# Squared norms of the delta rule's queries and keys: from GpSimd squares and products with ones to ScalarE sums over transposes

## The chip, the cores and the metric

The kernel runs on one core of a Trainium2 chip. The metric is the device time of one execution in microseconds. The engines of the core are TensorE (PE in the profile; its weight loads are PEld), VectorE (DVE), ScalarE (ACT), GpSimd (POOL) and SyncE (SP), each with its own queue of instructions, executed in order; they wait for each other through semaphores. TensorE writes to PSUM, the others read and write PSUM or SBUF, GpSimd SBUF alone.

## What is computed

A trunk of two residual layers over 256 tokens of 2048 channels, all in float32. The even layer projects the normalised input to three mixers (a gated delta rule of 8 heads, a long depthwise convolution behind a gated linear unit, and attention to 256 memory tokens), gates them, and projects back; the odd layer does the same with stick-breaking attention. What the change touches is the normalisation of the delta rule's queries and keys:

```python
def l2_norm(x):
    return x * lax.rsqrt(jnp.sum(x * x, axis=-1, keepdims=True) + EPS)

    qkv = jax.nn.silu(causal_depthwise_conv(qkv_a, conv_qkv)).astype(f32)
    q, k, v = [t.reshape(bsz, seq, DN_HEADS, DN_HEAD_DIM) for t in jnp.split(qkv, 3, axis=-1)]
    q = l2_norm(q) * (DN_HEAD_DIM ** -0.5)
    k = l2_norm(k)
    beta = jax.nn.sigmoid(b_a.astype(f32))
    g = -jnp.exp(a_log.astype(f32)) * jax.nn.softplus(a_a.astype(f32) + dt_bias.astype(f32))
    o = gated_delta_rule(q, k, v, beta, g)
```

## The kernel before

**The stream of weights.** All weight matrices are read once, in 432 chunks of 256 rows by 512 columns (512 KB), through six raw buffers. For each chunk ScalarE makes a rounded copy (`whi`, line 824), VectorE the remainder (`wlo`, line 1153), and TensorE twelve matmuls of 128x512 (lines 1497 to 1499: high by high, remainder by high, high by remainder, for two row blocks and two token blocks). `split` (ScalarE's and VectorE's part) of chunk c stands in the plan between chunks c-5 and c-4. A job is a group of chunks that yields 512 output columns; `evac` j copies its result to SBUF on ScalarE (line 851).

**The mixers between the chunks.** `make_plan` puts every step of the mixers into one list, in which the chunks are the clock: a stream of steps has a position in chunks, each step adds a cost in chunks, and the step goes ahead of the chunk at its rounded position. Each engine walks the list and issues its part of each step, so the list is the order of all queues. There is no other scheduler. A step that is not ready holds back everything behind it on its engine.

**The delta rule, group by group.** Heads 0 to 3 are group 0, heads 4 to 7 group 1. The four PSUM banks `mixer0` to `mixer3` (M[0] to M[3]) serve all steps; `take` makes TensorE wait until the last user of a bank has been read. For head h:

- `dnT`: TensorE turns q, k and v to channel order, six transposes into banks 0 and 1 (line 1517, the common helper of all transposes).
- `dnC`: ScalarE multiplies the last tap of the short convolution (line 918), VectorE adds the nine others (line 1227).
- `dnS`: ScalarE's tanh (lines 924, 925) into banks 0 and 1; `dnU`: VectorE's gate product (lines 1235, 1237), after which `ykqv` holds k, q and v. The next `dnT` waits for it.
- `dnB`: GpSimd squares k and q (line 743) into `scr`; TensorE multiplies the squares with ones, four products of one column each (line 1581), into columns 384 to 387 of bank 2, and turns k's first half and v's halves back to token order (three transposes); ScalarE copies them to `tok` (line 932), VectorE copies the four norms to `nrm` (line 1243).
- `dnV` for a whole group: VectorE adds a constant (line 1248), ScalarE takes the logarithm (line 936), VectorE makes the exponents (lines 1252 to 1265), ScalarE the exponential (line 938). Each of the two functions has a table load.
- `dnR`: TensorE turns the exponents, VectorE copies them to `rows`. `dnG`: TensorE's products of k and q and the decays (lines 1599 to 1607), ScalarE's exponential (line 946), VectorE's product (line 1282).
- `d4x` and `d4y`: the inverse by seven doubling levels, for two pairs of heads in turn (numbers 0 to 6 and 7 to 13 in group 0, 14 to 20 and 21 to 27 in group 1); GpSimd masks (line 763), TensorE multiplies (lines 1619, 1634, 1635), VectorE reads the banks (lines 1290 and 1291 for the first level, 1304 and 1305 later).
- `d5a` to `d5e`, `d6`, `gate` and `d7`: the outputs, their norm, their gate, and two transposes back (ScalarE's copy, line 988).

Beside it run `glu` (ScalarE's tanh, line 993, VectorE's product, line 1341), its transposes `gT`, the taps of the long convolution `conv` on VectorE (lines 1355 and 1358, four a step), and `za`, the gate of the delta rule (line 910, line 1215).

Of the kernel before, what the change touches and what calls it, by code (L numbers as in the profile page):

```python
# [129 lines left out]
DN_STEP = 3.5  # L130
# [13 lines left out]
def make_plan(last_job):  # L144
# [18 lines left out]
    def deltanet(g):  # L163
# [126 lines left out]
def prog(nc, x, mem, vecs, w, a_log, dt_bias, out, last_job=len(JOBS)):  # L290
# [4 lines left out]
    with ctx:  # L295
# [140 lines left out]
        s_sq = sem("dn_squares")  # L436
        s_back = sem("dn_kv_transposed_back")
        s_tok = sem("dn_kv_by_token")
        s_np = sem("dn_norms_summed")
        s_nrm = sem("dn_norms_copied")  # L440
# [99 lines left out]
        def banks(step, i):  # L540
            if step == "xt":
                return [i % 3 if 8 <= i < F_OB else i % 4]
            if step in ("mqT", "mkT"):
                return [i % 2]
            if step == "mao":
                return [2 + i % 2]
            if step == "d4y":
                return [] if i % 7 == 0 else ([1, 2] if i % 7 < 6 else [2])
            return {"first": [0], "vec": [3], "ba": [0], "bat": [1], "bas": [2], "dnT": [0, 1], "dnB": [2], "dnR": [1], "dnG": [0, 1],
                    "d4x": [0],  # L550
                    "d5a": [0], "d5b": [1], "d5c": [2], "d5d": [0], "d5e": [1], "d7": [2], "gT": [3], "zT": [3],
                    "lnm": [3], "lns": [3], "mas": [0], "mat": [1], "sbT": [0], "sbz": [1], "sbo": [2]}.get(step, [])
# [4 lines left out]
        def read(step, i):  # L557
# [3 lines left out]
                    "dnB": (s_nrm, i + 1), "dnR": (s_rows, i + 1), "dnG": (s_aq, i + 1),  # L561
# [134 lines left out]
        def _(gp):  # L696
# [105 lines left out]
            steps = {"rstd": do_rstd, "dnB": do_dnB, "dnG": do_dnG, "d4x": do_d4x, "lnc": do_lnc, "d6": do_d6, "sbk": do_sbk, "sbn": do_sbn,  # L802
# [6 lines left out]
        def _(sc):  # L809
# [311 lines left out]
            def do_xload(b):  # L1121
# [6 lines left out]
                     "za": do_za, "dnC": do_dnC, "dnS": do_dnS, "dnB": do_dnB, "dnV": do_dnV, "dnG": do_dnG, "d4x": do_d4x,  # L1128
# [13 lines left out]
        def _(ve):  # L1142
# [327 lines left out]
            def do_sbo(h):  # L1470
# [9 lines left out]
                     "dnU": do_dnU, "dnB": do_dnB, "dnV": do_dnV, "dnR": do_dnR, "dnG": do_dnG, "d4x": do_d4x,  # L1480
# [9 lines left out]
        def _(pe):  # L1490
# [85 lines left out]
            def do_dnB(h):  # L1576
                pe.wait_ge(s_silu, 2 * h + 2)
                take("dnB", h)
                pe.wait_ge(s_sq, h + 1)
                for a in range(4):  # L1580
                    ins = mm(M[2][:, 384 + a:385 + a], scr[:, 128 * a:128 * a + 128], ones[:, 0:1], start=True, stop=True)
                ins.then_inc(s_np, 1)
# [3 lines left out]
                turn(M[2][:, 256:384], y[:, 2, 128:256]).then_inc(s_back, 1)  # L1586

# [187 lines left out]
            def do_sbo(h):  # L1775
# [9 lines left out]
                     "dnT": do_dnT, "dnB": do_dnB, "dnR": do_dnR,  # L1785
# [49 lines left out]
```

## Time and profile before

| | us |
|---|---|
| median of three runs | 1425.14 |
| lowest and highest | 1423.98, 1425.86 |
| the profiled execution | 1425.36 |
| its span in the trace | 1423.6 |

| engine | busy us | share of the span |
|---|---|---|
| TensorE, matmuls | 1398.6 | 98% |
| TensorE, weight loads | 1167.6 | 82% |
| VectorE | 896.5 | 63% |
| ScalarE | 758.7 | 53% |
| GpSimd | 136.2 | 10% |

The span is the time from the first to the last instruction in the trace; the execution's own time is 1.8 us longer. In the chain that ended last TensorE has 91% of the span, the three matmul lines of the chunks 26% each. A share of busy time is an average over the whole span; the steps of the delta rule lie between 100 and 530 us.

### The profile page before, as it was taken

How to read it: one execution, taken by the hardware profiler on the slowest of the kernel's cores; microseconds unless marked ns; L12 is line 12 of the kernel's file. 1: busy time of each engine (PE TensorE's matmuls, PEld its weight loads, DVE VectorE, ACT ScalarE, POOL GpSimd, SP SyncE). 2: the span in 40 equal slices, each digit the busy share in tenths (PEclk: the TensorE clock that was granted, in tenths of full speed). 3: DMA queues.
4: the chain of work that ended last, by engine and by line, in shares of the span. 5: the costliest groups of instructions: out<-in, count | busy, mean ns of one | idle time of the engine just before them, and what ended most of it. 6: DMA issues, size and time to landing. Idle time of an engine off the chain costs nothing.

```text
span 1423.6 us, 18074 instructions
## 1 busy us (share of the span) xinstructions
PE 1398.6 (98%) x6811; PEld 1167.6 (82%) x6811; DVE 896.5 (63%) x1297; ACT 758.7 (53%) x1175; POOL 136.2 (10%) x135
## 2 busy tenths in 40 slices
PE   7999999999999999999999999999999999999998
PEld 5888889888889888878888788888888888888887
DVE  4447697777786789865566553655554645656563
ACT  4545633455533564666444545765765756655441
POOL 3001222110322010000000120020020020000000
PEclk9999999999999999999999999999999999999999
DMA  7555533455433486546455565455464564553552
GB/s 261 184 186 163 163 120 104 133 163 161 150 118 104 135 272 215 163 132 213 140 160 177 173 215 176 140 184 183 152 194 160 178 192 163 177 177 105 192 192 75
DMA packets 124847, 236.42 MB, mean 166 GB/s; under 512 B 9648, under 2 KB 10073, under 8 KB 124761
## 3 DMA queue, kind: packets, MB, share of 16 engines
q1 hardware_dynamic: 122585, 231.07, 51.2%
q10 hardware_dynamic: 2176, 4.19, 0.9%
q8 instruction: 55, 0.90, 0.3%
q14 instruction: 31, 0.25, 0.1%
HBM read 233.14 MB, written 2.10 MB: 165 GB/s over the span
## 4 chain that ended last, share of the span: by engine, by line
PE 91%; DVE 4%; ACT 2%; issue 1%; SPq 1%; DMA 0%; POOL 0%; DVEq 0%; ACTq 0%
PE job L1497 26%; PE job L1499 26%; PE job L1498 26%; PE mixer L1517 4%; PE mixer L1619 2%; PE mixer L1635 1%; PE mixer L1634 1%; DVE wlo L1153 1%; PE mixer L1749 1%; PE mixer L1729 1%; ACT whi L824 1%; DVE cvr L1358 1%; DVE reg L1227 1%; PE mixer L1767 0%; PE mixer L1780 0%
## 5 line engine op out<-in xcount | busy, mean ns | idle before, releaser
L1497 PE MATMUL job<-whi,xhi 128*128 128x512 f32 x1728 | 695.2, 402 | 0.2 <-DVE wlo L1153 0.2
L1153 DVE TENSOR_TENSOR wlo<-raw,whi 128x1024 fp32r<-128x1024 f32 x432 | 527.6, 1239 | 246.6 <-ACT whi L824 244.2
L1499 PE MATMUL job<-whi,xlo 128*128 128x512 f32 x1728 | 677.0, 392 | 0.0
L1498 PE MATMUL job<-wlo,xhi 128*128 128x512 f32 x1728 | 675.5, 391 | 0.0
L824 ACT ACTIVATE whi<-raw 128x1024 fp32r<-128x1024 f32 x432 | 445.4, 1056 | 135.9 <-PE job L1499 127.8
L1499 PEld LDWEIGHTS job<-whi,xlo 128*128 128x128 f32 x1728 | 325.7, 188 | 70.6
L1498 PEld LDWEIGHTS job<-wlo,xhi 128*128 128x128 f32 x1728 | 326.5, 189 | 62.7
L1497 PEld LDWEIGHTS job<-whi,xhi 128*128 128x128 f32 x1728 | 326.2, 189 | 62.7 <-issue 0.6
L1358 DVE SCALAR_TENSOR_TENSOR cvr<-cvr,vt 128x255 f32<-128x255 f32 (+14 forms) x240 | 117.3, 549 | 0.0
L851 ACT ACTIVATE proj<-job,rstd 128x512 f32<-128x512 f32 x80 | 50.5, 686 | 43.0 <-PE job L1499 35.5
L955 ACT ACTIVATE reg<-mixer 128x512 f32<-128x512 f32 x24 | 14.4, 599 | 93.0 <-PE mixer L1619 93.0
L1169 DVE TENSOR_TENSOR hid<-hid,job 128x512 f32<-128x512 f32 x48 | 30.8, 682 | 50.1 <-PE job L1499 50.1
L763 POOL TENSOR_TENSOR reg<-hid,mix 128x512 f32<-128x512 f32 x28 | 39.5, 1410 | 120.6 <-DVE mix L1305 87.3
L1517 PE MATMUL mixer<-ident,proj 128*128 128x128 f32 x256 | 42.3, 273 | 4.3 <-DVE proj L1419 2.5
L732 POOL TENSOR_TENSOR brs<-bss,mhalf 128x16 f32<-128x16 f32 x4 | 15.2, 3807 | 308.7 <-DVE bss L1449 308.7
L1455 DVE SCALAR_TENSOR_TENSOR scr<-mixer,scr 128x384 f32<-128x384 f32 x16 | 8.9, 558 | 56.4 <-ACT scr L1109 56.4
L1517 PEld LDWEIGHTS mixer<-ident,proj 128*128 128x128 f32 x256 | 32.0, 141 | 14.7 <-issue 3.3
L1107 ACT ACTIVATE scr<-mixer 128x384 f32<-128x384 f32 x16 | 7.9, 492 | 60.0 <-PE mixer L1767 60.0
L1227 DVE SCALAR_TENSOR_TENSOR reg<-mixer,vt,reg 128x255 f32<-128x255 f32 (+2 forms) x72 | 28.8, 473 | 11.2 <-ACT reg L918 11.1
L1635 PE MATMUL mixer<-mix,reg 128*128 128x64 f32 x192 | 34.9, 273 | 0.0
L861 ACT ACTIVATE xhi<-mixer,vt 128x256 fp32r<-128x256 f32 x48 | 20.0, 471 | 25.4 <-PE mixer L1517 25.4
L1174 DVE SCALAR_TENSOR_TENSOR xlo<-mixer,vt,xhi 128x256 fp32r<-128x256 f32 x48 | 20.8, 478 | 14.3 <-ACT xhi L861 14.3
(253 smaller groups left out, 976.1 us busy)
## 6 DMA issues: line engine op xcount, KB each, us to landing
raw<-in_od_w_in_dram SPq DMA_DIRECT2D x160, 512.0 KB, 4.4
raw<-in_ev_w_in_dram SPq DMA_DIRECT2D x144, 512.0 KB, 3.7
raw<-in_ev_w_out_dram SPq DMA_DIRECT2D x48, 512.0 KB, 4.6
raw<-in_od_w_out_dram SPq DMA_DIRECT2D x48, 512.0 KB, 4.4
raw<-in_w_mem_kv_dram SPq DMA_DIRECT2D x32, 512.0 KB, 4.1
hid<-in_x_dram SPq DMA_DIRECT2D x4, 512.0 KB, 7.6
reg<-in_mem_dram ACTq DMA_DIRECT2D x4, 512.0 KB, 6.0
hid<-in_x_dram ACTq DMA_DIRECT2D x4, 512.0 KB, 7.9
```

Source lines behind the costliest of these rows:

```text
L763: nc.gpsimd.tensor_tensor(ofx[:, par, :, :], aq[:, 4 * par:4 * par + 4, 0, :], level[:, l, :].unsqueeze(1).broadcast_to([128, 4, 128]), AL ...
L824: act(whi[:, c % RING, :, :], raw[:, c % RAWS, :, :], ACT.Copy).then_inc(s_hi, 1)
L851: ins = act(dst, pj[j % 2][t][:, :], ACT.Copy, scale=rstd[:, src, t:t + 1])
L1153: vec.tensor_tensor(wlo[:, c % RING, :, :], raw[:, c % RAWS, :, :], whi[:, c % RING, :, :].bitcast(F32), ALU.subtract).then_inc(s_lo, 1)
L1169: ins = vec.tensor_tensor(v, v, pj[j % 2][t][:, :], ALU.add)
L1227: vec.scalar_tensor_tensor(out=y[:, r:], in0=dn_source(c)[:, 0:S - r], scalar=vt[:, col:col + 1], in1=y[:, r:], op0=ALU.mult, op1=ALU.add) ...
L1358: ins = vec.scalar_tensor_tensor(out=c[:, d:], in0=gsrc[:, 0:S - d], scalar=vt[:, col:col + 1], in1=c[:, d:], op0=ALU.mult, op1=ALU.add)
L1497: mm(out_, xh, hi, start=first, stop=False)
L1498: mm(out_, xh, lo, start=False, stop=False)
L1499: return mm(out_, xl, hi, start=False, stop=last)
L1517: return nc.tensor.transpose(dst, src, ident[:, :])
L1635: ins = mm(m2, ofx[:, par, m, :], t1[:, :, 1, :], start=True, stop=True)
```

## The change

`dnB` is split. TensorE no longer multiplies squares with ones and GpSimd no longer squares. `dnB` on TensorE is the three transposes alone, and ScalarE, ahead of its copy to `tok`, squares k's first half where it lies in bank 2 and sums along the row into `nrm` (`accum_out`). A new step `dnE` turns the other three halves (k's second, q's both) into bank 2, and ScalarE squares and sums each. VectorE's copy of the norms is gone. In the plan `dnB` of a head no longer stands in front of the next head's `dnT` but one step earlier, `dnE` takes its place, and the cost of `dnU` and the wait at the group's end are shorter, so that what follows in the delta rule stands one chunk earlier in group 0 and one to two chunks earlier in group 1. The numbers of `nrm` keep their meaning.

```diff
@@ make_plan, deltanet(g) @@
         for h in range(h0, h0 + 4):
-            s += [(("dnT", h), .2), (("dnC", h), 1.2), (("dnS", h), .9), (("dnU", h), DN_STEP - 2.1)]
+            s += [(("dnT", h), .2), (("dnC", h), 1.2)]
             s += [(("dnB", h - 1), .1)] if h > h0 else []
-        s += [("wait", 1), (("dnB", h0 + 3), 1), (("dnV", g), 2), (("dnR", g), 2.2)]
+            s += [(("dnS", h), .9), (("dnU", h), DN_STEP - 2.3)]
+            s += [(("dnE", h - 1), .1)] if h > h0 else []
+        s += [("wait", .5), (("dnB", h0 + 3), 1), (("dnE", h0 + 3), .5), (("dnV", g), 2), (("dnR", g), 2.2)]
         s += [(("dnG", h), 1) for h in range(h0, h0 + 4)]
@@ who has read a bank @@
-                    "dnB": (s_nrm, i + 1), "dnR": (s_rows, i + 1), "dnG": (s_aq, i + 1),
+                    "dnB": (s_tok, i + 1), "dnE": (s_nrm, i + 1), "dnR": (s_rows, i + 1), "dnG": (s_aq, i + 1),
@@ GpSimd @@
-            def do_dnB(h):
-                gp.wait_ge(s_silu, 2 * h + 2)
-                if h:
-                    gp.wait_ge(s_np, h)
-                k = ykqv[:, h % 4, 0:2, :]
-                nc.gpsimd.tensor_tensor(scr[:, 0:512].rearrange("p (c s) -> p c s", c=2), k, k, ALU.mult).then_inc(s_sq, 1)
-
@@ ScalarE @@
                 sc.wait_ge(s_ss, 1)
+                act(scr[:, 0:128], M[2][:, 0:128], ACT.Square, accum_out=nrm[:, h, 0:1])
                 act(tok[:, h % 4, :, :], M[2][:, 0:384].rearrange("p (c n) -> p c n", c=3), ACT.Copy).then_inc(s_tok, 1)
+
+            def do_dnE(h):
+                sc.wait_ge(s_kq, h + 1)
+                for a in range(1, 4):
+                    ins = act(scr[:, 128 * a:128 * a + 128], M[2][:, 128 * a - 128:128 * a], ACT.Square,
+                              accum_out=nrm[:, h, a:a + 1])
+                ins.then_inc(s_nrm, 1)
@@ VectorE @@
-            def do_dnB(h):
-                ve.wait_ge(s_np, h + 1)
-                ve.wait_ge(s_tok, h + 1)
-                vec.tensor_copy(nrm[:, h, :], M[2][:, 384:388]).then_inc(s_nrm, 1)
-
@@ TensorE @@
                 take("dnB", h)
-                pe.wait_ge(s_sq, h + 1)
-                for a in range(4):
-                    ins = mm(M[2][:, 384 + a:385 + a], scr[:, 128 * a:128 * a + 128], ones[:, 0:1], start=True, stop=True)
-                ins.then_inc(s_np, 1)
                 y = ykqv[:, h % 4, :, :]
                 turn(M[2][:, 0:128], y[:, 0, 0:128])
                 turn(M[2][:, 128:256], y[:, 2, 0:128])
                 turn(M[2][:, 256:384], y[:, 2, 128:256]).then_inc(s_back, 1)
+
+            def do_dnE(h):
+                take("dnE", h)
+                y = ykqv[:, h % 4, :, :]
+                turn(M[2][:, 0:128], y[:, 0, 128:256])
+                turn(M[2][:, 128:256], y[:, 1, 0:128])
+                turn(M[2][:, 256:384], y[:, 1, 128:256]).then_inc(s_kq, 1)
```

What the new order is, at three places. First ScalarE at the end of group 0, from the work on head 3's norms to the first copy of a GLU transpose. `hln` holds the logarithms, `ex` the factors, `proj` in the row with 1024 columns the GLU's gate, `whi<-raw` a chunk's rounded copy. Before:

```order
L932 ACTIVATE hid<-mixer2 128x384
L993 ACTIVATE proj<-proj 128x1024
L824 ACTIVATE whi<-raw 128x1024
L936 ACT_TABLE_LOAD
L936 ACTIVATE hln<-hln 128x16
L938 ACT_TABLE_LOAD
L938 ACTIVATE ex<-ei 128x32
L997 ACTIVATE cvr<-mixer3 128x256
```

and with the change:

```order
L932 ACTIVATE scr,nrm<-mixer2 128x128 x3
L938 ACT_TABLE_LOAD
L938 ACTIVATE hln<-hln 128x16
L940 ACT_TABLE_LOAD
L940 ACTIVATE ex<-ei 128x32
L995 ACTIVATE proj<-proj 128x1024
L818 ACTIVATE whi<-raw 128x1024
L999 ACTIVATE cvr<-mixer3 128x256
```

The GLU's tanh has moved from ahead of the logarithm and the exponential to behind them. TensorE's GLU transposes stand one chunk behind head 3's last transposes in both.

Second, VectorE from the product of `dnG` with which `za` shares its place to the first read of the inverse (`mix<-ident,mixer0`), group 0. `hid<-mixer0,hid` is a head's `dnG`, `cvr<-cvr,vt` are taps of the long convolution. Before:

```order
L1282 TENSOR_TENSOR hid<-mixer0,hid 128x512
L1215 SCALAR_TENSOR_TENSOR mix<-mix,proj 128x2x512
L1358 SCALAR_TENSOR_TENSOR cvr<-cvr,vt 128x252 x2
L1358 SCALAR_TENSOR_TENSOR cvr<-cvr,vt 128x251 x2
L1153 TENSOR_TENSOR wlo<-raw,whi 128x1024
L1282 TENSOR_TENSOR hid<-mixer0,hid 128x512
L1358 SCALAR_TENSOR_TENSOR cvr<-cvr,vt 128x250 x2
L1358 SCALAR_TENSOR_TENSOR cvr<-cvr,vt 128x249 x2
L1153 TENSOR_TENSOR wlo<-raw,whi 128x1024
L1290 TENSOR_TENSOR mix<-ident,mixer0 128x512
```

and with the change:

```order
L1279 TENSOR_TENSOR hid<-mixer0,hid 128x512
L1217 SCALAR_TENSOR_TENSOR mix<-mix,proj 128x2x512
L1355 SCALAR_TENSOR_TENSOR cvr<-cvr,vt 128x252 x2
L1355 SCALAR_TENSOR_TENSOR cvr<-cvr,vt 128x251 x2
L1155 TENSOR_TENSOR wlo<-raw,whi 128x1024
L1355 SCALAR_TENSOR_TENSOR cvr<-cvr,vt 128x250 x2
L1355 SCALAR_TENSOR_TENSOR cvr<-cvr,vt 128x249 x2
L1155 TENSOR_TENSOR wlo<-raw,whi 128x1024
L1287 TENSOR_TENSOR mix<-ident,mixer0 128x512
```

The last head's `dnG` has moved ahead of `za`, out of this stretch; the taps and remainders in it are the same. In the plan `d4x` 0 and 7 keep their chunks (51, 52), `d4x` 1 moves from chunk 54 to 53.

Third, VectorE in group 1, from the last exponents (`ei<-hln`) to the product of head 4 (`hid<-mixer0,hid`). Before:

```order
L1265 TENSOR_SCALAR ei<-hln 128x8
L1215 SCALAR_TENSOR_TENSOR mix<-mix,proj 128x2x512
...
L1277 TENSOR_SCALAR nks<-ex 128x8
L1358 SCALAR_TENSOR_TENSOR cvr<-cvr,vt 128x228 x2
L1358 SCALAR_TENSOR_TENSOR cvr<-cvr,vt 128x227 x2
L1153 TENSOR_TENSOR wlo<-raw,whi 128x1024
L1358 SCALAR_TENSOR_TENSOR cvr<-cvr,vt 128x226 x2
L1153 TENSOR_TENSOR wlo<-raw,whi 128x1024
L1282 TENSOR_TENSOR hid<-mixer0,hid 128x512
```

and with the change:

```order
L1262 TENSOR_SCALAR ei<-hln 128x8
L1355 SCALAR_TENSOR_TENSOR cvr<-cvr,vt 128x234 x2
...
L1274 TENSOR_SCALAR nks<-ex 128x8
L1217 SCALAR_TENSOR_TENSOR mix<-mix,proj 128x2x512
L1355 SCALAR_TENSOR_TENSOR cvr<-cvr,vt 128x230 x2
L1355 SCALAR_TENSOR_TENSOR cvr<-cvr,vt 128x229 x2
L1155 TENSOR_TENSOR wlo<-raw,whi 128x1024
L1355 SCALAR_TENSOR_TENSOR cvr<-cvr,vt 128x228 x2
L1355 SCALAR_TENSOR_TENSOR cvr<-cvr,vt 128x227 x2
L1155 TENSOR_TENSOR wlo<-raw,whi 128x1024
L1279 TENSOR_TENSOR hid<-mixer0,hid 128x512
```

`za` has moved behind the copies of `dnR`, and the two last taps (128x226) now follow the product.

## Rows read from the trace of the kernel before

**Rows 1.** The page's busy shares, us (share of the span) xinstructions.

```profile
PE 1398.6 (98%) x6811; PEld 1167.6 (82%) x6811; DVE 896.5 (63%) x1297; ACT 758.7 (53%) x1175; POOL 136.2 (10%) x135
```

**Rows 2.** The chain that ended last: start us, us, what; head 0's norms.

```profile
123.15 0.79 PE mixer L1581 x8
123.94 1.04 PE mixer L1517 x9
```

**Rows 3.** Timeline, 150 to 172: start, us, engine, line, op, tiles [idle before <-releaser].

```profile
153.79 0.49 ACT L932 ACTIVATE hid<-mixer 128x384 f32<-128x384 f32 x1 [2.48 <-PE mixer L1517]
...
155.26 1.23 DVE L1341 SCALAR_TENSOR_TENSOR proj<-proj 128x1024 f32<-128x1024 f32 x1 [0.72 <-ACT proj L993]
...
156.20 1.28 ACT L936 ACT_TABLE_LOAD   x1
...
156.54 0.44 PE L1517 MATMUL mixer<-ident,proj 128*128 128x128 f32 x2
...
157.74 0.22 ACT L936 ACTIVATE hln<-hln 128x16 f32<-128x16 f32 x1 [0.26 <-DVE hln L1248]
```

**Rows 4.** Timeline of ScalarE at a pair of squares with sums.

```profile
276.71 0.31 ACT L983 ACTIVATE hid<-hid 128x128 f32<-128x128 f32 x1 [1.92 <-DVE hid L1316]
...
277.31 0.35 ACT L973 ACTIVATE scr<-mixer,ex 128x128 f32<-128x128 f32 x1
```

**Rows 5.** Timeline of TensorE: the transposes of heads 0 and 1.

```profile
101.46 0.82 PE L1517 MATMUL mixer<-ident,proj 128*128 128x128 f32 x6
...
111.41 0.85 PE L1517 MATMUL mixer<-ident,proj 128*128 128x128 f32 x6 [0.96 <-DVE reg L1237]
```

**Rows 6.** Timelines of TensorE, then VectorE: `dnG` 3, `d4x` 0 and 7, group 0.

```profile
181.72 1.02 PE L1599 MATMUL mixer<-reg 128*128 128x256 f32 x4
...
183.16 0.45 PE L1497 MATMUL job<-whi,xhi 128*128 128x512 f32 x1
...
185.95 1.05 PE L1619 MATMUL mixer<-ident,reg 128*128 128x128 f32 x8
...
190.53 1.13 PE L1619 MATMUL mixer<-ident,reg 128*128 128x128 f32 x8 [0.80 <-DVE mix L1291]
...
189.71 0.68 DVE L1291 TENSOR_TENSOR mix<-ident,reg 128x512 f32<-128x512 f32 x1
...
194.61 0.68 DVE L1291 TENSOR_TENSOR mix<-ident,reg 128x512 f32<-128x512 f32 x1
```

**Rows 7.** Timelines of ScalarE, VectorE, TensorE: from `dnB` 7 to `dnG` 5.

```profile
355.11 1.26 ACT L851 ACTIVATE proj<-job,rstd 128x512 f32<-128x512 f32 x2
...
357.35 1.23 DVE L1153 TENSOR_TENSOR wlo<-raw,whi 128x1024 fp32r<-128x1024 f32 x1 [0.38 <-ACT whi L824]
...
364.88 1.31 DVE L1215 SCALAR_TENSOR_TENSOR mix<-mix,proj 128x1024 f32<-128x1024 f32 x1 [1.60 <-ACT mix L910]
...
374.77 0.81 DVE L1358 SCALAR_TENSOR_TENSOR cvr<-cvr,vt 128x226 f32<-128x226 f32 x2
...
376.64 0.68 DVE L1282 TENSOR_TENSOR hid<-mixer,hid 128x512 f32<-128x512 f32 x1
...
358.08 0.53 PE L1517 MATMUL mixer<-ident,reg 128*128 128x128 f32 x3
...
377.46 1.10 PE L1599 MATMUL mixer<-reg 128*128 128x256 f32 x4 [0.85 <-DVE hid L1282]
```

**Rows 8.** Waits of TensorE: line <- waited for: us in total, times, longest.

```profile
PE mixer L1517 <- ACT mix L988: 0.7, 1, 0.7
```

**Rows 9.** Timeline of TensorE; then stretches: busy of engines, PEclk, DMA share, GB/s.

```profile
25.25 0.66 PE L1517 MATMUL mixer<-ident,hid 128*128 128x128 f32 x2 [3.51 <-DVE xlo L1174]
...
634.02 0.44 PE L1517 MATMUL mixer<-ident,proj 128*128 128x128 f32 x2 [2.53 <-DVE proj L1419]
...
25.00:31.00 6.00, 5.75 (x15) 4.50 (x16) 3.62 (x6) 1.91 (x4) 0.00 (x0) 0.50 1.05 387
635.00:640.00 5.00, 5.00 (x18) 3.94 (x17) 4.64 (x5) 3.68 (x8) 0.00 (x0) 0.66 0.56 173
```

More of the change, by code:

```diff
@@ L435, in prog @@
         s_silu = sem("dn_silu")
-        s_sq = sem("dn_squares")
         s_back = sem("dn_kv_transposed_back")
         s_tok = sem("dn_kv_by_token")
-        s_np = sem("dn_norms_summed")
-        s_nrm = sem("dn_norms_copied")
+        s_kq = sem("dn_kq_transposed_back")
+        s_nrm = sem("dn_norms_summed")
         s_lnq = sem("dn_log_norms")
@@ L548, in banks @@
                 return [] if i % 7 == 0 else ([1, 2] if i % 7 < 6 else [2])
-            return {"first": [0], "vec": [3], "ba": [0], "bat": [1], "bas": [2], "dnT": [0, 1], "dnB": [2], "dnR": [1], "dnG": [0, 1],
+            return {"first": [0], "vec": [3], "ba": [0], "bat": [1], "bas": [2], "dnT": [0, 1], "dnB": [2], "dnE": [2], "dnR": [1], "dnG": [0, 1],
                     "d4x": [0],
@@ L800, in do_sbn @@
                                             ALU.mult).then_inc(s_sbn, 1)
-            steps = {"rstd": do_rstd, "dnB": do_dnB, "dnG": do_dnG, "d4x": do_d4x, "lnc": do_lnc, "d6": do_d6, "sbk": do_sbk, "sbn": do_sbn,
+            steps = {"rstd": do_rstd, "dnG": do_dnG, "d4x": do_d4x, "lnc": do_lnc, "d6": do_d6, "sbk": do_sbk, "sbn": do_sbn,
                      "mqs": lambda i: mq_power(i, order[i]), "mks": lambda i: mq_power(4 + i, order[4 + i])}
@@ L1127, in _ @@
                      "baw": do_baw, "ba": do_ba, "bat": do_bat,
-                     "za": do_za, "dnC": do_dnC, "dnS": do_dnS, "dnB": do_dnB, "dnV": do_dnV, "dnG": do_dnG, "d4x": do_d4x,
+                     "za": do_za, "dnC": do_dnC, "dnS": do_dnS, "dnB": do_dnB, "dnE": do_dnE, "dnV": do_dnV, "dnG": do_dnG, "d4x": do_d4x,
                      "d5a": do_d5a, "d5b": do_d5b, "d5c": do_d5c, "d5d": do_d5d, "d5e": do_d5e, "d7": do_d7,
@@ L1479, in _ @@
                      "za": do_za, "dnC": do_dnC,
-                     "dnU": do_dnU, "dnB": do_dnB, "dnV": do_dnV, "dnR": do_dnR, "dnG": do_dnG, "d4x": do_d4x,
+                     "dnU": do_dnU, "dnV": do_dnV, "dnR": do_dnR, "dnG": do_dnG, "d4x": do_d4x,
                      "d4y": do_d4y, "d5c": do_d5c, "d5e": do_d5e, "d6": do_d6, "gate": do_gate, "glu": do_glu,
@@ L1784, in _ @@
             steps = {"chunk": do_chunk, "xt": do_xt, "vec": do_vec, "ba": do_ba, "bat": do_bat, "bas": do_bas,
-                     "dnT": do_dnT, "dnB": do_dnB, "dnR": do_dnR,
+                     "dnT": do_dnT, "dnB": do_dnB, "dnE": do_dnE, "dnR": do_dnR,
                      "dnG": do_dnG, "d4x": do_d4x, "d4y": do_d4y, "d5a": do_d5a, "d5b": do_d5b, "d5c": do_d5c,
```

## The prediction

> **What bounds the kernel now.** First the page's busy shares: TensorE is busy for 1398.6 of 1423.6 us [rows 1]; the engine whose queue never empties is the bound, and anything else counts only where TensorE comes to wait for it. So I read the waits of TensorE next, then the chain that ended last for what its instructions cost in that queue, then the timelines of ScalarE, VectorE and TensorE at the few places where the new order leaves TensorE less time between asking and needing. "Chunk n" is the group of twelve weight matmuls between two mixer steps; it costs 2.79 us (183.16 to 185.95) [rows 6]. The profiled execution took 1425.4 us, 0.2 above the median of the three runs; the sum is made against it.
>
> **Part 1: work on TensorE.** Removed for each of eight heads: the four products with ones, eight instructions in 0.79 us of the chain [rows 2]. Added: three more transposes. Nine stand in 1.04 us [rows 2], 0.35 for three; as they now stand alone more often, I take 0.38. The upper bound is two in 0.44, so 0.66 for three [rows 3]. Gain: 8 x (0.79 - 0.38) = 3.3 us, between 1.0 and 3.5. GpSimd's eight squares and VectorE's eight copies of the norms go too; TensorE never waited for the copies, so I cost their loss at nothing. The loads of the memory input and of x, issued from ScalarE's queue, move a chunk or two forward together with the steps around them; TensorE never waits for them, cost nothing; the queue of the weight loads keeps its order.
>
> **Part 2: ScalarE's squares, and who queues behind them.** ScalarE gets 32 squares with a sum. Two such squares with their read-outs take 276.71 to 277.31, 0.60 us, so 0.30 each [rows 4]; the bound above is instruction plus read-out end to end, 0.5. In most places they fall into ScalarE's idle time. The dear place is the end of the first group. Before, the copy of head 3 was followed by the GLU's tanh, then VectorE's GLU product; TensorE's first GLU transpose came at 156.54, 0.05 us after the product ended at 155.26 + 1.23 = 156.49 [rows 3]. There is no slack. Now ScalarE does the three squares, a table load, the logarithm, a second load and the exponential, and only then the tanh; VectorE likewise has its exponents ahead of the GLU product (the order of both engines shows it). TensorE's distance from head 3's last transposes to the GLU transpose is one chunk, as before. So the tanh is later by 0.90 (squares) + 2 x 1.28 (loads) + 2 x 0.22 (logarithm, exponential) - 0.49 (the copy that stood there) = 3.4 us [rows 3, 4]. With 0.14 us from VectorE's end to TensorE's start (189.71 + 0.68 to 190.53 [rows 6]) and the 0.05 slack, TensorE waits 3.5 us, between 2.6 (squares for nothing) and 4.1 (squares at 0.5).
>
> The row shows a load of 1.28 us at 156.20, ended by 157.48, and the logarithm at 157.74 behind a VectorE step [rows 3]. The Trainium skill, "ScalarE: Activation LUTs", section "What ACT_TABLE_LOAD costs", adds a drain of some 1.38 us to every load; by it the wait would be 2.8 us longer. The trace leaves 0.26 us behind the load, against that rule, and the sum goes by the row.
>
> **Part 3: less room between transposes.** dnT of heads 3 and 7 now comes three chunks after that of the head before, not four. One such spacing exists: dnT 0 at 101.46, dnT 1 at 111.41 with 0.96 us of waiting [rows 5]: the convolution, tanh and product round trip takes 9.95, TensorE's own work 8.99. In the new places TensorE also has three groups of three transposes, 8.99 + 3 x 0.38 = 10.13. The round trip starts after dnE (0.38), and the squares outlast dnT's own transposes by 0.90 - (1.04 - 0.38) = 0.24, so it takes 10.57. Wait 0.44, twice: 0.9 us, between 0 and 1.9 (the 0.96 each).
>
> **Part 4: first products of the inverse, first group.** Step d4x 7 waited 0.80 us at 190.53 for VectorE to read the bank of d4x 0 [rows 6]. Now dnG 3 lies a chunk earlier, so TensorE asks 1.44 us sooner (181.72 to 183.16), and VectorE is freed of only one product ahead, 0.68 [rows 6, 7]: wait 0.80 + 1.44 - 0.68 = 1.56. Then d4x 1, before two chunks behind d4x 7, stands one behind: TensorE is there after 1.13 + 2.79 = 3.92 us, VectorE reads that bank 4.90 after the former (189.71 to 194.61) [rows 6]; wait 0.98. Together 2.5 against 0.8: 1.7 us more, between 0 and 2.4.
>
> **Part 5: second group's decay matrices.** dnG 5 waited 0.85 us at 377.46 for the product of dnG 4 [rows 7]. Now dnV 1 follows dnE 7 at once, and everything to dnG 5 comes a chunk sooner after the last transposes: TensorE asks at 377.46 - 0.85 - 358.08 - 2.79 = 15.7 us after their start. VectorE: 0.52 (transposes, hand-over) + 0.90 (squares) + 3.00 (loads, logarithm, exponential) + 2.24 (job result and split on ScalarE until VectorE's split, 355.11 to 357.35) = 6.7; then its queue to dnG 4, which ran 364.88 to 376.64, 11.76 us without a gap, now without the last two taps of 0.81: 17.6. From that product's start to TensorE 0.82: 18.4. Wait 2.7, 1.8 more than before, between 0 and 2.4 more.
>
> **Part 6: back.** The last output transposes, which stood two steps in one chunk and waited 0.7 us [rows 8], get a chunk each: 0.7 us gained.
>
> **Part 7: TensorE's clock.** Behind a wait of 2.53 us the granted clock was 0.66 over the stretch 635 to 640, so partly at the lower of the two levels (1.2 GHz), price 0.34 x 5 = 1.7 us; behind one of 3.51 us it was 0.50 over 25 to 31, price 0.50 x 6 = 3.0 [rows 9]. Part 2's wait of 3.5 us is like the larger; I take the middle of the two prices, 2.4 us. Part 5's 2.7 us is barely above 2.53; I count nothing and keep 1.7 for the range.
> The Trainium skill has the rule, "TensorE: Matmul & The Clock Gate", section "Why this matters for your kernels": an idle gap between bursts of matmuls puts the engine back to half rate. It speaks against this change, and both rows agree with it.
>
> Sum: -3.3 + 3.5 + 0.9 + 1.7 + 1.8 - 0.7 + 2.4 = 6.3. 1425.4 + 6.3 = **1431.7 us**.
>
> **Rivals.**
> (a) *The shorter queue wins.* Price: 3.3 + 0.7 less of TensorE's time, 1425.4 - 4.0 = 1421.4. It needs the GLU product to be ready within 1.2 us of TensorE's asking (4.0 - 1.2 = 2.8, the bound of "faster"); up to there the change gains. For it: TensorE is 98% busy and really gets less work, and VectorE no longer stands in wait for the norms. Against it: the queue order at the GLU step is fixed, and its two loads alone are 2.6 us. Chance 0.08.
> (b) *One wait, one gain.* Only part 2's wait comes, parts 3 to 5 are covered since VectorE is freed of its blocking copies, and the clock holds: 1425.4 - 4.0 + 3.5 = 1424.9; with the clock's smaller price 1426.6. For it: the waits of 0.8 to 1.0 us are small against 2.79 us a chunk. Against it: VectorE's stretches in parts 4 and 5 have no gap that a copy caused. Chance 0.20.
> (c) *The clock falls twice*, after parts 2 and 5, at 3.0 and 1.7: 1425.4 + 3.9 + 4.7 = 1434.0. Chance 0.12.
> (d) *A table load holds ScalarE for longer than its instruction shows*, say once more its own 1.28 us: two loads on the way, at part 2 and at part 5, 4 x 1.28 = 5.1 more, 1425.4 + 6.3 + 5.1 = 1436.8. The 0.26 us in the row speaks against it. Chance 0.02.
> This is the mechanism of the drain in the Trainium skill, "ScalarE: Activation LUTs", weighed above.
> That the change doesn't do what it says can be excluded by the order: products and GpSimd squares are gone, and ScalarE has as many table loads as before.
>
> **The numbers.** The forecast has 0.58, (a) 0.08, (b) 0.20, (c) 0.12, (d) 0.02. A measurement tells 0.2%, 2.8 us, from no change, so "same" is 1422.3 to 1428.0. (a) is faster, (b) is same, the rest slower: 0.08, 0.20, 0.72. The range: all low ends with the smaller price of the clock give 1425.4 - 3.5 + 2.6 - 0.7 + 1.7 = 1425.5, the foot; it leaves out (a) and the lower half of (b). All high ends give 1425.4 - 1.0 + 4.1 + 1.9 + 2.4 + 2.4 - 0.7 + 4.7 = 1439.2, which hardly come together; 1437 takes in (c) and most of what is above it.
>
> **What would show it.** In the changed profile: a wait of TensorE's first GLU transpose for VectorE's product of about 3.5 us near 155; a clock window under 1.0 behind it; dnT 3 and dnT 7 waiting some 0.4 us for VectorE's gate product; two waits for the inverse's first copies near 190; one of 2.7 us at dnG 5; no wait at the output transposes; 32 squares at 0.3 us on ScalarE. If the GLU wait is under 1 us, the forecast falls; if it is there and the total is still at 1425, parts 3 to 5 were covered.

## The result, and the profile of the changed kernel

| | us |
|---|---|
| changed kernel, median of seven executions | 1429.41 (1428.58 to 1433.86) |
| kernel before, beside it | 1425.14 |
| ratio | 1.0041, 95% interval 1.0031 to 1.0052 |
| changed kernel, the profiled execution | 1428.66, span 1426.7 |

The change costs 4.3 us, 0.4%. The forecast was 1431.7 in a range of 1425.5 to 1437.0. The page's busy shares [rows 1]:

```profile
PE 1395.1 (98%) x6771; PEld 1162.2 (81%) x6771; DVE 894.5 (63%) x1289; ACT 766.9 (54%) x1239; POOL 126.9 (9%) x127
```

TensorE is busy for 3.5 us less and the kernel is slower, so the whole loss lies in the time in which it stands idle: 31.6 us of the span against 25.0 before. The view of TensorE's waits (line, line waited for, us in total, times, longest) has:

```profile
PE mixer L1514 <- DVE proj L1338: 3.6, 1, 3.6
PE mixer L1514 <- DVE reg L1239: 2.9, 4, 1.2
PE mixer L1599 <- DVE hid L1279: 2.8, 1, 2.8
PE mixer L1619 <- DVE mix L1288: 2.7, 2, 1.7
...
PE mixer L1514 <- DVE mix L1395: 1.1, 1, 1.1
PE mixer L1514 <- DVE proj L1416: 0.7, 1, 0.7
PE mixer L1514 <- ACT mix L990: 0.6, 1, 0.6
```

The same waits before (the line numbers there are a few off): GLU no wait, `dnT` 1.4 in two, decay matrices 0.85, inverse 0.80, the `mix` of line 1395 none, the late `proj` 2.53 [rows 9]. The last row, 0.6 for ScalarE's `mix`, is the wait of `dnB` 4 for bank 2 (at 329.00), which was 0.61 before; the output transposes' 0.7 [rows 8] is gone. The GLU place, which answers to [rows 3], in the timeline (start, us, engine, line):

```profile
151.36 0.28 ACT L932 ACTIVATE scr<-mixer 128x128 f32<-128x128 f32 x1 [1.39 <-PE mixer L1514]
...
151.63 0.27 ACT L932 ACTIVATE scr<-mixer 128x128 f32<-128x128 f32 x1
...
151.88 0.28 ACT L932 ACTIVATE scr<-mixer 128x128 f32<-128x128 f32 x1
...
152.26 1.28 ACT L938 ACT_TABLE_LOAD   x1
...
153.56 0.21 ACT L938 ACTIVATE hln<-hln 128x16 f32<-128x16 f32 x1
...
153.79 1.28 ACT L940 ACT_TABLE_LOAD   x1
...
155.09 0.23 ACT L940 ACTIVATE ex<-ei 128x32 f32<-128x32 f32 x1
155.22 1.04 ACT L995 ACTIVATE proj<-proj 128x1024 f32<-128x1024 f32 x1
156.29 1.32 DVE L1338 SCALAR_TENSOR_TENSOR proj<-proj 128x1024 f32<-128x1024 f32 x1 [1.60 <-ACT proj L995]
...
157.67 0.44 PE L1514 MATMUL mixer<-ident,proj 128*128 128x128 f32 x2 [3.59 <-DVE proj L1338]
```

Read it from the bottom: TensorE waits 3.59 us for VectorE's product, that for ScalarE's tanh, and the tanh starts when both table functions and three squares are through. From the first square to the tanh ScalarE hardly pauses, 3.86 us. The second load starts 0.02 us behind the logarithm, the logarithm 0.02 behind the first load: no hidden time behind either. The other waits in TensorE's timeline (`dnT` 3, 5 and 7; `d4x` 7 and 1; `dnG` 5), answering to [rows 5 to 7]:

```profile
132.67 0.84 PE L1514 MATMUL mixer<-ident,proj 128*128 128x128 f32 x6 [0.37 <-DVE reg L1239]
...
192.10 1.13 PE L1619 MATMUL mixer<-ident,reg 128*128 128x128 f32 x8 [1.66 <-DVE mix L1288]
...
197.01 1.13 PE L1619 MATMUL mixer<-mix,reg 128*128 128x128 f32 x8 [1.04 <-DVE mix L1288]
...
315.82 0.85 PE L1514 MATMUL mixer<-ident,proj 128*128 128x128 f32 x6 [1.24 <-DVE reg L1239]
...
339.45 0.85 PE L1514 MATMUL mixer<-ident,proj 128*128 128x128 f32 x6 [0.36 <-DVE reg L1239]
...
376.24 1.10 PE L1599 MATMUL mixer<-reg 128*128 128x256 f32 x4 [2.80 <-DVE hid L1279]
```

The row at 315.82 is `dnT` 5, which the forecast had left out. The clock, in stretches (start:end, length, busy of the engines, PEclk):

```profile
20.00:31.00 11.00, 8.35 (x37) 6.64 (x36) 5.26 (x8) 5.21 (x9) 0.00 (x0) 0.84 1.03 384
31.00:370.00 339.00, 329.24 (x1714) 276.46 (x1712) 233.66 (x388) 177.90 (x333) 34.05 (x36) 1.00 0.49 149
370.00:390.00 20.00, 17.20 (x85) 14.12 (x84) 13.76 (x21) 8.32 (x15) 7.83 (x10) 0.91 0.51 152
390.00:1420.00 1030.00, 1025.34 (x4888) 853.51 (x4887) 632.36 (x860) 566.72 (x870) 72.18 (x43) 1.00 0.53 168
```

In this execution the clock stayed at 2.4 GHz behind the GLU wait, and also near 635, where it fell before and where the wait is now 0.7 us. It was at 1.2 GHz for part of the time behind `dnG` 5.

### The profile page after: what moved, and what is told of

Read it like the earlier page. It is cut to its first block, busy times and chain, and to the rows that moved or that the text cites. A ratio compares the mean times of both kernels' runs of the same rounds, so it can differ in the third digit from the quotient of the medians.

```text
span 1426.7 us, 18027 instructions
## 1 busy us (share of the span) xinstructions
PE 1395.1 (98%) x6771; PEld 1162.2 (81%) x6771; DVE 894.5 (63%) x1289; ACT 766.9 (54%) x1239; POOL 126.9 (9%) x127
## 4 chain that ended last, share of the span: by engine, by line
PE 90%; DVE 5%; ACT 2%; SPq 1%; issue 1%; DMA 0%; POOL 0%; DVEq 0%; ACTq 0%
PE job L1494 26%; PE job L1496 26%; PE job L1495 25%; PE mixer L1514 4%; PE mixer L1619 2%; DVE wlo L1155 2%; PE mixer L1635 1%; PE mixer L1634 1%; PE mixer L1749 1%; PE mixer L1729 1%; DVE reg L1229 1%; DVE cvr L1355 1%; ACT whi L818 1%; PE mixer L1767 0%; PE mixer L1780 0%
## 5 line engine op out<-in xcount | busy, mean ns | idle before, releaser
L1355 DVE SCALAR_TENSOR_TENSOR cvr<-cvr,vt 128x255 f32<-128x255 f32 (+14 forms) x240 | 114.2, 535 | 0.0
```

Source lines behind the costliest of these rows:

```text
L1355: ins = vec.scalar_tensor_tensor(out=c[:, d:], in0=gsrc[:, 0:S - d], scalar=vt[:, col:col + 1], in1=c[:, d:], op0=ALU.mult, op1=ALU.add)
```

## Experiments

Two theories stood against each other: the loss is the sum of four waits that the order brings (the forecast), or the new method itself, ScalarE's squares, is what costs. In the diffs `move(a, b)` takes step a out of the finished plan and puts it ahead of b, and `put(a, c)` puts it behind chunk c. Each ratio is to the kernel before run beside the experiment: its median was 1424.84 us (27 executions) for the first four and 1424.57 us (15) for the four behind them.

**One wait alone: the GLU step ahead of head 3's squares.**

```diff
+    move(("glu", 0), ("dnE", 3))
```

> The changed kernel with one move in the plan: glu 0 (ScalarE's tanh, VectorE's product) stands ahead of dnE 3 and dnV 0 instead of behind them. Theory of the waits: TensorE's 3.6 us of waiting at the first GLU transpose go, nothing takes their place, the other waits stay (two at the gate products of about 0.4, 1.7 and 1.0 at the inverse, 2.8 at dnG 5): 1429.4 - 3.6 = 1425.8 us, and the executions above 1431 us are gone. Rival, the clock: the loss is mostly the granted clock that falls behind a wait; the fall behind dnG 5 stays, and the time stays at 1428 or above. Rival, hidden anyway: what is gained at the GLU comes back as a longer wait at dnR, dnG or the inverse within the next ten chunks, time 1429.

Measured: 1424.45 us (1423.25 to 1424.98), ratio to before 0.9997 (0.9989 to 1.0006). One step moved past three squares and two table functions gives back 5.0 us between the medians, and no execution of eleven is above 1425.0. The GLU row is gone from TensorE's waits; the others stand where they were:

```profile
PE mixer L1519 <- DVE reg L1244: 3.0, 4, 1.3
PE mixer L1604 <- DVE hid L1284: 2.8, 1, 2.8
PE mixer L1624 <- DVE mix L1293: 2.7, 2, 1.7
```

In the two profiled executions the gain is 1426.7 - 1422.9 = 3.8 us, the wait (3.6) and nothing of the clock, since it had not fallen there. That the medians give 1.2 more is the first sign that it does fall there in other executions.

**The method alone: ScalarE's sums with all other steps at their old places.**

```diff
@@ make_plan, deltanet(g): the streams of before @@
+    for h, b, e in ((0, 33, 34), (1, 37, 38), (2, 39, 40), (3, 41, 42), (4, 87, 88), (5, 91, 92), (6, 93, 94), (7, 95, 96)):
+        if (b, h) not in ((33, 0), (37, 1), (87, 4), (91, 5)):
+            put(("dnB", h), b)
+        put(("dnE", h), e)
```

> The method of the change (four squares with sums on ScalarE, six transposes, no products with ones, no GpSimd squares) with the plan of the kernel before for all other steps. dnB 0, 1, 4, 5 keep their chunks, dnB 2, 3, 6, 7 come one or two chunks sooner, each dnE stands one chunk behind its dnB, dnE 3 behind glu 0. Theory of the waits: TensorE gets 3.3 us less work and has the waits of the kernel before (0.96, 0.80, 0.85, 0.7): 1425.1 - 3.3 = 1421.8 us. Rival, the method costs: the squares and the second hand-over on ScalarE delay the splits and the gate products, and the time is 1425 or above, with new waits at dnT.

Measured: 1420.98 us (1420.60 to 1423.58), ratio 0.9977 (0.9968 to 0.9986). In the old order the new method is worth 3.9 us; with the new order that gain is lost and 4.3 us more. All four waits of the forecast are back at their old size:

```profile
PE mixer L1522 <- DVE proj L1424: 2.5, 1, 2.5
PE mixer L1522 <- ACT scr L940: 1.8, 2, 0.9
...
PE mixer L1522 <- DVE reg L1247: 1.4, 2, 1.0
...
PE mixer L1607 <- DVE hid L1287: 0.9, 1, 0.9
PE mixer L1627 <- DVE mix L1296: 0.8, 1, 0.8
```

The second row is new, and two of its kind: `dnB` 2 and `dnB` 6 want bank 2 while the squares of the head before are not done.

**The order alone: before's method in the changed plan.** GpSimd's squares and the products with ones stay, `dnE` is an empty step, and the plan is the changed one.

> The kernel before (GpSimd squares, products with ones) in the changed plan, in which dnE does nothing. Theory of the waits: TensorE's work is as before, the norms are there a chunk sooner than in the changed kernel, so the GLU wait is only about 1.2 us, that at dnG 5 under 1 and those at dnT 3 and 7 near 0; the waits at the inverse (1.7 and 1.0) and the gain at the output transposes do not depend on the squares and stay: 1425.1 + 1.2 + 1.9 - 0.7 - 0.3 = 1427 us. Rival, the plan alone: the waits belong to the plan and none to the squares; then all of them stay and 3.3 us of TensorE's work come on top: 1432.7 us.

Measured: 1425.38 us (1425.04 to 1426.36), ratio 1.0006 (0.9997 to 1.0015). The wait of the inverse stayed at its full size and that of the GLU step came near the expected 1.2. At `dnG` 5, where less than 1 was expected, it is 1.4:

```profile
PE mixer L1621 <- DVE mix L1293: 2.7, 2, 1.7
...
PE mixer L1519 <- DVE reg L1239: 2.2, 2, 1.2
PE mixer L1519 <- DVE proj L1343: 1.5, 1, 1.5
...
PE mixer L1601 <- DVE hid L1284: 1.4, 1, 1.4
...
PE mixer L1519 <- DVE proj L1421: 0.7, 1, 0.7
```

The time is 1.6 us under the expectation, and the last row gives the likely reason: the late wait is 0.7 here as in the changed kernel, not 2.5. The order has a gain in its tail that the forecast had put at nothing. It also shows that the two halves of the change do not add up: the order alone costs nothing, the method alone gains 3.9, together they lose 4.3. The method puts squares ahead of the table functions in a place where the order has just put those ahead of the tanh. This kernel and the changed one have the same plan, so their difference is what the method does in it. From chunk 24 to 128 the changed kernel, in an execution whose clock did not fall there, takes 403.11 us against 401.63 here, while TensorE's waits in that stretch sum to 12.6 against 7.8 us (2.1 more at the GLU step, 1.4 at `dnG` 5, 0.7 at `dnT` 3 and 7, 0.6 at `dnB` 4). So in the changed plan the method saves TensorE 3.3 us of work, adds 4.8 us of waits, and in most executions adds a fall of the clock as well.

**One cost doubled: every square of `dnE` twice.**

```diff
                 for a in range(1, 4):
+                    act(reg[:, 2944 + 128 * a:3072 + 128 * a], M[2][:, 128 * a - 128:128 * a], ACT.Square,
+                        accum_out=wnrm[:, h, a:a + 1])
                     ins = act(scr[:, 128 * a:128 * a + 128], M[2][:, 128 * a - 128:128 * a], ACT.Square,
```

> The changed kernel, with dnE's three squares done twice (the extra three write to a place that nobody reads): 0.9 us more on ScalarE in each dnE. Theory of the waits: each wait behind dnE grows by 0.9: GLU 3.6 to 4.5, gate products 0.37 to 1.3 twice, dnG 5 2.8 to 3.7, the inverse unchanged; 1429.4 + 3.6 = 1433.0 us. Rival: ScalarE's time is not on the path of the waits (the table loads and the order alone make them), and the time stays within 1 us of 1429.4. The clock may add 1.7 to 3 us in single executions in both.

Measured: 1433.62 us (1432.82 to 1434.50), ratio 1.0062 (1.0049 to 1.0076).

```profile
PE mixer L1517 <- DVE reg L1242: 4.4, 4, 1.3
PE mixer L1517 <- DVE proj L1341: 4.4, 1, 4.4
...
PE mixer L1602 <- DVE hid L1282: 2.8, 1, 2.8
...
PE mixer L1602 <- DVE rows L1274: 0.6, 1, 0.6
```

The expectation was 1433.0. The GLU wait grows by 0.8 us, and the three extra squares hold ScalarE for 0.8 there (1.67 us from the first square to the table load, against 0.90): at this place ScalarE's queue counts one for one. The wait at `dnG` 5 was expected at 3.7 and stayed at 2.8. The last row is where the rest went: `dnG` 4 now waits 0.6 us for the copied rows, one step ahead. VectorE's queue shifted as a whole, as the forecast had it, but TensorE had only a little room left before an earlier step met it. 0.6 + 2.8 = 3.4 is near the 3.7. The `dnT` waits grew by 1.5, from 2.9 to 4.4. In all the waits grew by 2.9 us, not by 3.6, and the median by 4.2. That the total met the expectation is therefore partly chance; the profiled execution has a fall of the clock at both places (0.89 in 154 to 170 and in 374 to 390), where the one of 1428.66 has one.

**Three short waits taken out of the old order.** The kernel with the old places, and

```diff
+    move(("dnE", 1), ("dnS", 3))
+    move(("dnE", 5), ("dnS", 7))
+    move(("dnB", 4), ("chunk", 88))
+    move(("d7", 7), ("conv", 56))
```

> ScalarE's sums in the old plan (as in the run with the old places), with three short waits taken away by order alone: the three squares of heads 1 and 5 stand ahead of the next head's tanh on ScalarE (TensorE waited 0.93 and 0.90 us for them, since they stood behind a tanh that itself waited for VectorE), head 4's transposes stand behind those of head 6 (0.66), and the last output transpose has a chunk of its own (0.7). Theory (a wait of TensorE is all that these orders cost): 1421.0 - 1.8 - 0.7 - 0.7 = 1417.8 us, the rows gone from TensorE's waits. Rival (the squares ahead of the tanh delay the gate product, 0.9 us each, and the next transposes wait instead): 1419.5 to 1421, with new waits for the gate product's register.

Measured: 1418.75 us (1418.22 to 1419.70), ratio 0.9957 (0.9945 to 0.9970). It is 0.9 us above the expected 1417.8. The rows for `scr` and ScalarE's `mix` are gone. The two waits for squares and that of `dnB` 4 gave their time back (chunks 39, 93 and 87 are 1.1, 1.1 and 0.65 us shorter). The output transpose in a chunk of its own gave nothing: chunk 137 is 1.1 us shorter, and chunks 138 to 146 are 1.1 longer together, with a new wait of 0.3 for VectorE's `xlo`. This is what was in the way of the squares, in ScalarE's timeline of the kernel with the old places:

```profile
140.23 0.60 ACT L926 ACTIVATE mixer<-reg 128x512 f32<-128x512 f32 x1 [2.71 <-DVE reg L1237]
...
141.07 0.26 ACT L940 ACTIVATE scr<-mixer 128x128 f32<-128x128 f32 x1
```

ScalarE stood idle for 2.71 us ahead of a tanh, and for the last 1.8 us of it the data of the squares behind it was ready (TensorE's `dnE` 1 stands at 137.91, 0.49 us). A ready instruction behind one that waits is what the new order cures. The squares' length has a part in it too: they start at 141.07, TensorE asks for the bank at 141.15, and its wait of 0.93 is the time that they take.

**The tail a chunk earlier.** The same kernel, and `lnc` 6 to `lno` 7 with `zT` 8 to 15 (the norm and the output transposes of the long convolution, chunks 148 to 170) one chunk earlier, as the changed plan has them.

> The same, and in addition the steps of the long convolution's norm and its output transposes (chunks 148 to 170) stand one chunk earlier, as the change has them and the plan before has not. My prediction gave this shift nothing. In the changed kernel TensorE's wait for VectorE's scaled keys near 635 us was 0.7 instead of 2.5 us, and a new one of 1.1 us stood near 580. Theory (the shift is what shortened the late wait, because VectorE is done with the work of those steps before the keys' squares come): 0.7 to 1.8 us less than the kernel beside it, so 1416.0 to 1417.1, and less often a fall of the clock at 635 (1.7 us when there is one). Rival (it came from elsewhere, for instance from loads that moved with the second group): the wait of 2.5 stays and the two kernels agree within 0.5 us.

Measured: 1417.38 us (1416.68 to 1417.89), ratio 0.9947 (0.9934 to 0.9959). It is the fastest version, 7.2 us under the kernel before and 12 under the changed one's first median. The late wait of 2.5 is gone from the rows altogether; one of 0.5 stands at `mix`. So the shift of the tail is the cause of the late gain, not the loads or the second group. The median gain is 1.4 us, inside the expected 0.7 to 1.8. The mechanism, read from ScalarE's timeline of before:

```profile
628.54 0.42 ACT L1018 ACTIVATE cvr<-cvr 128x256 f32<-128x256 f32 x1 [1.62 <-DVE cvr L1388]
...
629.81 0.40 ACT L1047 ACTIVATE scr<-proj 128x256 f32<-128x256 f32 x1
```

The squares of the keys (`scr<-proj`) stand right behind `lno` 7 (`cvr<-cvr`), which waits 1.62 us for VectorE. In the changed kernel that `lno` comes 2.5 us earlier, counted from the start of chunk 174, and the squares 1.6 earlier. Once more a step in wait held back a ready one.

**The queue ahead of `dnG` 5 shortened.** The first experiment's kernel, and

```diff
+    move(("za", 1), ("chunk", 100))
+    for q in (("conv", 31), ("lnc", 2), ("lnc", 3)):
+        move(q, ("chunk", 102))
```

> The changed kernel with the GLU step ahead of head 3's squares (1424.45 us), and VectorE's queue ahead of head 4's product in group 1 shortened by 2.8 us: the delta rule's gate step stands behind that product, one convolution step stands two chunks later. TensorE's wait of 2.8 us at the second decay matrices should go. Theory with the clock (in the profiled execution it fell for 3.4 us right behind this wait, price 1.7): 1424.5 - 2.8 - 1.7 = 1420.0, no fall near 375. Theory without the clock (it falls elsewhere or as often as before): 1421.7. Rival (VectorE's moved work comes due at once behind it, at the third decay matrices or the GLU transposes of group 1): 1423 to 1424.5.

Measured: 1422.99 us (1422.34 to 1423.15), ratio 0.9986 (0.9977 to 0.9995).
My edit was only half of what I had meant. `conv` 31 already stood behind the product, so that only the gate step (1.2 us) left the queue, and TensorE's wait for the product went from 2.8 to 1.6, not to nothing. The median fell by 1.5, of which 1.2 are this wait; the profiled executions differ by 2.6, and this one had no fall of the clock behind 31 us, where the first experiment's had one behind its 2.8 (0.91 in 374 to 390). Both theories named numbers for a wait that was gone, so neither is settled by this; how the clock's share varies is what the next runs show.

**The changed kernel itself, four executions more with a profile.** The seven times of the result fell into two groups, so what differs between executions of one program was the question.

> The changed kernel itself, unaltered, for more executions and a second profile, because its seven times so far fall into two groups, 1428.6 to 1429.4 at a mean granted clock of 0.996 to 0.997 and 1431.6 to 1433.9 at 0.992 to 0.995. If the clock falls behind its waits in some executions and not in others, times again spread over 1428 to 1434, a lower mean clock goes with a longer time at 1.7 us for each 3.4 us at half clock, and the second profile may show the fall behind the GLU wait near 158 us that the first did not. If the spread came from anything else, long and short executions have the same mean clock. Median 1429 to 1431.

> The changed kernel once more, one profiled execution. Its twelve timed executions lie between 1427.7 and 1433.9 us with mean granted clocks from 0.998 down to 0.992; the two profiled ones (0.997 and 0.998) had no fall behind the 3.6 us GLU wait, one of them had one behind the 2.8 us wait. Theory (the clock falls behind a given wait in some executions only, each fall some 3.4 us at half clock): an execution of 1431 us or more shows two to four more falls, behind the GLU wait near 158, the waits of the inverse near 192 or the decay matrices near 377; one of 1429 us or less shows none or one of these. Rival (a different cause, spread over the whole span): no more than two falls in a long execution.

> The same kernel and the same question as the run before it: where the granted clock falls in a third execution with a profile.

> The same kernel and the same question again: where the granted clock falls in a further execution with a profile.

Measured in the first: median 1431.47 us (1427.73 to 1432.33), ratio 1.0045 (1.0031 to 1.0059), the profiled execution being the shortest. The median is a little above the expected 1429 to 1431, and a lower mean clock goes with a longer time, 0.998 at 1427.73 down to 0.992 at 1433.55, as expected. The other three: 1431.26, 1432.48 and 1433.55. The waits of TensorE agree to 0.1 us in all of them (GLU 3.6, decay matrices 2.8, inverse 2.7), but for that on the input at the start. The stretches from 154 to 170 and from 374 to 390 do not. In the execution of 1427.73:

```profile
154.00:170.00 16.00, 12.39 (x63) 9.93 (x62) 8.04 (x17) 8.71 (x14) 7.26 (x12) 1.00 0.48 141
374.00:390.00 16.00, 13.22 (x71) 10.95 (x70) 11.29 (x16) 6.86 (x12) 8.62 (x10) 1.00 0.56 165
```

in that of 1431.26:

```profile
154.00:170.00 16.00, 12.39 (x51) 9.61 (x51) 8.05 (x17) 8.20 (x12) 7.23 (x12) 0.89 0.42 129
374.00:390.00 16.00, 13.21 (x60) 10.60 (x59) 12.65 (x17) 5.91 (x10) 6.65 (x9) 0.89 0.43 123
```

and in that of 1433.55:

```profile
154.00:170.00 16.00, 12.39 (x47) 9.57 (x46) 7.79 (x17) 8.08 (x12) 7.19 (x12) 0.79 0.38 117
374.00:390.00 16.00, 13.20 (x54) 10.54 (x53) 12.13 (x18) 5.80 (x11) 6.68 (x9) 0.79 0.43 125
```

The column to read is the granted clock (1.00, 0.89, 0.79), and with it the count of matmuls: TensorE is busy for the same 12.39 us, but issues 63, 51 and 47. The starts of chunks in the trace give the price. From chunk 40 to 48 (around the GLU wait) and from 96 to 104 (around `dnG` 5):

| execution, us | 40 to 48 | 96 to 104 | PEclk there |
|---|---|---|---|
| 1427.73 | 30.77 | 31.74 | 1.00, 1.00 |
| 1428.66 | 30.74 | 33.32 | 1.00, 0.89 |
| 1431.26 | 32.34 | 33.24 | 0.89, 0.89 |
| 1432.48 | 33.24 | 34.68 | 0.79, 0.79 |
| 1433.55 | 33.28 | 34.75 | 0.79, 0.79 |

A stretch at 0.89 costs 1.5 to 1.6 us, one at 0.79 costs 2.5 to 3.0. The two places together explain 0, 1.6, 3.1, 5.4 and 5.5 us. What is left is the clock at the start, which fell for longer in the executions of 1427.73, 1431.26 and 1433.55 (0.9 to 1.0 us at chunk 24): without both, the five times are 1426.9, 1427.1, 1427.2, 1427.0 and 1427.1. The falls at these two waits, with the start, are the whole spread of six microseconds. By its own sign (no more than two falls in a long execution) my rival was not refuted, since each long one has exactly two; it is out because these two leave at most 0.3 us unexplained. Of the theory two things were wrong: behind the waits of the inverse the clock never fell, and a fall is not always of one length, since 0.79 stands for twice the time at half clock that 0.89 does. What decides in a single execution whether the clock falls, no run here shows.

## Why the prediction was right, and where it was not

The forecast was 1431.7; the median was 1429.4, in the executions taken later 1431.5. Steps in the prediction's order, in the profiled execution of 1428.66 where nothing else is said:

| part | forecast | measured |
|---|---|---|
| 1, TensorE's work | -3.3 | -3.3 (against before's method in the same plan); busy time -3.5, with the clock in it |
| 2, GLU wait | +3.5 | +3.59 |
| 3, `dnT` 3 and 7 | +0.9 | +0.7; `dnT` 5 +0.8 |
| 4, inverse (1.56 and 0.98 against 0.80) | +1.7 | +1.9 (1.66 and 1.04) |
| 5, `dnG` 5 (2.7 against 0.85) | +1.8 | +1.95 |
| 6, output transposes | -0.7 | -0.7 (0.7 and 0.6 before, 0.6 now) |
| not in the forecast: the tail | 0 | -1.8 + 1.1 |
| 7, clock | +2.4, behind the GLU | 0 there, +1.6 behind `dnG` 5, near 635 -1.7 priced as in [rows 9] or -1.4 by the starts of chunks 174 to 178 |

**Parts 1 to 6** were worked out from the durations of single instructions and from who stands behind whom, and came within 0.2 us each. The sum without the clock was 3.9. It can be tested in one line: the execution of 1427.73 had no fall of the clock behind 31 us, and before, with its fall near 635 taken off (0.34 x 5 = 1.7 [rows 9], or 1.4), is at 1423.7 to 1424.0; the difference is 3.7 to 4.1. That is the sum of 3.9, but it holds two misses that nearly cancel, +0.8 at `dnT` 5 and -0.7 in the tail. At the start both lost about the same (0.25 us apart at chunk 24). The granted clock of the execution of 1427.73:

```profile
31.00:700.00 669.00, 654.60 (x3389) 551.53 (x3388) 476.46 (x782) 354.25 (x656) 70.93 (x68) 1.00 0.51 159
700.00:1420.00 720.00, 717.16 (x3305) 592.73 (x3304) 403.60 (x487) 399.40 (x563) 43.14 (x20) 1.00 0.53 168
```

**Part 2's table loads**: 1.28 us each and 0.02 behind them. The Trainium skill, "ScalarE: Activation LUTs", section "What ACT_TABLE_LOAD costs", adds a drain of some 1.38 us per load. It is not there in this kernel; by it the wait would have been some 6.4 us (an estimate from that figure), and it was 3.59. Rival (d) falls with it.

**Part 1** depends on the neighbours, which I had not seen. Where `dnB` or `dnE` stand alone, three transposes lengthen a chunk by 0.37 (2.72 to 3.09 us from chunk to chunk), where they stand beside a `dnT` by 0.25 to 0.33. In the kernel without the short waits the sum over heads is larger: from chunk 24 to 128 it takes 391.13 us against 395.89 before; of the 4.8 us, 0.6 are the wait of `dnB` 4 and 0.6 stand at the chunks of the first two GLU transposes (43 and 44), of which the view of waits shows 0.2. The chunks of the norms themselves are 3.8 shorter, above my upper bound of 3.5; some 0.2 is lost again at `dnG` 5. In the changed plan the work saved is the 3.3 of the third experiment, as forecast.

**Part 3** was right on the two steps it named and missed a third. `dnT` 5 was three chunks behind `dnT` 4 before as well, so I took it as unchanged. But in the new plan three gate steps stand on VectorE directly ahead of head 4's taps, where one stood:

```profile
304.73 0.60 DVE L1331 SCALAR_TENSOR_TENSOR hid<-hid,ofac,mix 128x128 f32<-128x128 f32 x2
...
306.39 1.65 DVE L1331 SCALAR_TENSOR_TENSOR hid<-hid,ofac,mix 128x128 f32<-128x128 f32 x6
307.97 3.59 DVE L1229 SCALAR_TENSOR_TENSOR reg<-mixer,vt,reg 128x255 f32<-128x255 f32 x9
```

The taps start at 307.97, 2.87 us after `dnT` 4 (305.10); before, 307.06 and 304.97, 2.09. The 0.78 between them is the growth of the wait, from 0.46 to 1.24.

**The tail** was the sentence that failed: loads and steps around them "move a chunk or two forward", "cost nothing". No row of TensorE's waits names the loads that moved, that holds; but the same shift also freed ScalarE ahead of the late wait of 2.53 us, which I had quoted [rows 9] only for its clock. The step that I should have walked was what stands ahead of that wait.

**Part 7** had the mechanism right and gave it a certainty that it lacks. The price was a good one: 2.4 forecast, 0, 1.6 or 2.5 measured behind the GLU wait. At `dnG` 5 I counted nothing, on the ground that 2.7 is barely above 2.53; but 2.53 is a wait behind which the clock did fall, so that it argued for a price of 1.7, and 1.5 to 3.0 came in four of five profiled executions. Rival (c), the clock falling at both, had a chance of 0.12 and is what three of the five show. The Trainium skill has the rule in "TensorE: Matmul & The Clock Gate", section "Why this matters for your kernels": an idle gap between bursts of matmuls brings the engine back to half rate. The traces agree with it in seven of ten cases and bound it: behind the same gap of 3.6 us the clock fell in three executions and stayed in two, behind 2.8 us it fell in four of five, and never behind 1.66 us.

So the total was close for a reason that is partly luck: the tail's -0.7 and the clock's gain near 635 (1.4 to 1.7) stood against +0.8 at `dnT` 5 and the clock at `dnG` 5.

## What to carry to other kernels

When a step moves to an engine that has a strict queue, read that queue at each of its places for two things: what stands behind it that another engine is about to need, and whether it stands itself behind an instruction that waits. Here one step's place (GLU ahead of three squares and two table loads) was worth 5 us, and the places of two heads' squares 1.8. Where nothing waited behind them the squares cost nothing. Try a new method in the old order first, since the two can be worth +3.9 and nothing apart and lose 4.3 together; and price a wait of several microseconds on TensorE with its clock, as a cost that comes in some executions and not in others.

## What the runs showed of the hardware that was not expected

- The clock's response to an identical wait varies between executions: behind 3.6 us of idleness the 16 us that contain it were granted 1.00, 1.00, 0.89, 0.79 and 0.79, at a price of 0, 0, 1.6, 2.5 and 2.5 us. Behind the wait doubled in its squares (4.4 us) the one profiled execution was at 0.89.
- Three squares with sums, 128 columns each, back to back: 0.25 to 0.27 us from start to start, the read-out of 0.19 to 0.21 of each lying under the next square; with the last read-out 0.88 us for three. The pair in [rows 4] has 0.30 each.
- Four products with a single column and three transposes took 1.09 us of TensorE's stream (3.81 less 2.72 from chunk to chunk), three transposes alone 0.37. The products with one column are eight instructions for some 0.7 us, 0.09 each, against 0.12 for a transpose that streams 128 columns: few columns save little.
